# Products of constants in the gaps of TensorE: routing, the first expert, and the norms of the third block

## The reference, cut to what matters

```
x = layer_norm(ALPHA * x + mixer(x), ln1_g, ln1_b)         # second block
# routing: 4 groups, the best 2 of the 8 experts of the best group
lg = x @ wg + bg;  le = x @ we + be;  w = softmax(top 2) * p_top
# each of 32 experts, on the rows that chose it
y[rows] += ((silu(x[rows] @ w1) * (x[rows] @ w3)) @ w2) * w
x = layer_norm(ALPHA * x + y, ln2_g, ln2_b)
h = rms_norm(x, norm_gain_3);  proj = h @ w_in_3           # third block
```

## Time and profile before

| | us |
|---|---|
| median of 3 runs | 3408.27 (3405.32 to 3410.0) |
| the profiled execution, its own time | 3407.77 |
| its span in the profile | 3406.0 |
| routing, from the barrier to the next one | about 2373.9 to 2422.6 |
| third block's norms, barrier to first product | about 3019.4 to 3059.2 |

### The profile page before, as it was taken

The page is one execution under the profiler, slowest core; times in us unless marked ns, Lnnn a source line. Parts: engine busy times, 40 slices in busy tenths (PEclk is TensorE's granted clock), DMA queues, the critical chain, the costliest instruction groups (busy, mean ns, idle before and its releaser), DMA issues. The chain is left out here.

```text
span 3406.0 us, 34603 instructions
## 1 busy us (share of the span) xinstructions
PE 3016.5 (89%) x11712; PEld 1972.7 (58%) x11712; DVE 2402.0 (71%) x4782; ACT 1395.6 (41%) x2332; POOL 700.2 (21%) x583
## 2 busy tenths in 40 slices
PE   7999999977787777777789999997699999949999
PEld 4676644433333333333357898776588888837777
DVE  4888566667777776777759765545688889864675
ACT  2334222222222222222235423443488888853764
POOL 0000133344444444444410000000022212100000
PEclk9999999999999999899899999999799999969999
DMA  8432399999999999999962211343799999942212
GB/s 289 136 87 97 138 380 391 393 402 421 421 419 418 409 419 421 411 416 411 415 253 81 63 44 53 109 161 106 270 358 373 377 372 371 368 148 56 62 44 75
DMA packets 351924, 905.87 MB, mean 266 GB/s; under 512 B 29826, under 2 KB 170626, under 8 KB 285571
## 3 DMA queue, kind: packets, MB, share of 16 engines
q0 software_dynamic: 84000, 549.52, 39.5%
q1 hardware_dynamic: 267746, 354.11, 30.5%
HBM read 896.71 MB, written 31.99 MB: 273 GB/s over the span
## 5 line engine op out<-in xcount | busy, mean ns | idle before, releaser
L257 PE MATMUL peer_acc<-peer_uv,peer_diag 128*128 128x512 f32 x2048 | 992.9, 637 | 240.8 <-ACT peer_diag L313 238.4
L257 PEld LDWEIGHTS peer_acc<-peer_uv,peer_diag 128*128 128x128 f32 x2048 | 407.1, 203 | 808.0 <-issue 485.8
L434 DVE CUSTOM_DVE_ANT_0 peer_uv<-peer_uv,firsts_h 128x1024 f32<-128x1024 f32 x512 | 627.9, 1228 | 343.2 <-DMA peer_uv<-in_peer_uv,peer_experts 340.9
L208 POOL DMA_INDIRECT peer_uv<-in_peer_uv,peer_experts x512 | 575.6, 1124 | 1153.7 <-PE peer_acc L257 716.7
L3074 DVE TENSOR_TENSOR slotted_low<-slotted_raw,slotted_high 128x2048 fp32r<-128x2048 f32 x192 | 434.2, 2289 | 65.0 <-ACT slotted_high L3023 64.9
L3023 ACT ACTIVATE slotted_high<-slotted_raw 128x2048 fp32r<-128x2048 f32 x192 | 365.6, 1921 | 62.5 <-PE slotted_h L2980 50.2
L313 ACT ACTIVATE peer_diag<-all_consts,peer_weights 128x128 f32<-128x128 f32 x512 | 166.7, 391 | 333.1 <-DVE peer_weights L427 301.4
L304 ACT ACTIVATE peer_act_in<-peer_act_in 128x4 f32<-128x4 f32 (+2 forms) x131 | 26.8, 205 | 607.1 <-DVE peer_act_in L434 607.1
L2980 PE MATMUL slotted_h<-slotted_high,slotted_xT_high 128*128 128x512 f32 x512 | 204.7, 400 | 6.2 <-DVE slotted_low L3074 4.1
L2980 PE MATMUL slotted_h<-slotted_high,slotted_xT_low 128*128 128x512 f32 x512 | 201.6, 394 | 0.0
L2980 PE MATMUL slotted_h<-slotted_low,slotted_xT_high 128*128 128x512 f32 x512 | 201.2, 393 | 0.0
(11 more groups left out here) (758 smaller groups left out, 5597.4 us busy)
## 6 DMA issues: line engine op xcount, KB each, us to landing
slotted_raw<-in_moe_w SPq DMA_DIRECT2D x192, 1024.0 KB, 8.6
mixers_raw<-in_w_in SPq DMA_DIRECT2D x56, 512.0 KB, 3.8
firsts_ada_raw<-in_w_ada SPq DMA_DIRECT2D x64, 256.0 KB, 2.8
third_raw<-in_w_in SPq DMA_DIRECT2D x30, 512.0 KB, 3.6
firsts_raw<-in_w_in SPq DMA_DIRECT2D x28, 512.0 KB, 4.0
firsts_ada_first<-in_w_ada SPq DMA_DIRECT2D x8, 1024.0 KB, 13.9
peer_uv<-in_peer_uv,peer_experts POOLq DMA_INDIRECT x512, 10.7
ffn_w_raw<-in_peer_wq SPq DMA_DIRECT2D x10, 512.0 KB, 20.5
```

The lines of the kernel that those rows point to most:

```text
L208: pool.indirect_dma_start(uv[:, n % R, :, :].rearrange("p a d -> p (a d)"), None, A["peer_uv"], bass.IndirectOffsetOnAxis(ap=experts[:, si ...
L257: mm = nc.tensor.matmul(acc[t % 2][j][:, :], diag[:, n % 4, :], uv[:, n % R, 1, j * BANK:(j + 1) * BANK], start=(m == 0), stop=(m == E - 1))
L434: nc.vector.tensor_tensor_reduce(uv[:, n % R, 0, :], uv[:, n % R, 0, :], h2[:, t, :], 1.0, 0.0, ALU.mult, ALU.add, act_in[:, side, i:i + 1 ...
```

## The change

A helper multiplies two constant tiles of 128x128, `ones` and `ident`, into the first 128 columns of a bank `n` times. No one reads the result. Calls with fixed counts stand between the steps of TensorE.

```diff
+def idle_products(nc, C, bank, n):
+    for _ in range(n):
+        nc.tensor.matmul(bank[:, 0:P], C["ones"], C["ident"], start=True, stop=True)
 def routing(...):     # rows_tensor
             yield float(n)
+            if half == 0:
+                idle_products(nc, C, banks[n], (50, 8, 8, 14)[t])
             pe.wait_ge(x_ready, t + 1)
...                    # router_tensor
         yield 40.0
+        pe.wait_ge(x_low, 1)
+        idle_products(nc, C, banks[0], 14)
         pe.wait_ge(x_low, 2 * NT)
...
         tr.then_inc(lg_turned, 1)
+        idle_products(nc, C, banks[5], 36)
         pe.wait_ge(hits_ready, 1)
...
+        idle_products(nc, C, banks[5], 28)
         pe.wait_ge(at_ready, 1)
...                    # slotted_experts, TensorE
+                idle_products(nc, C, ps_x[0], 26)
                 turn_x(0)
+                idle_products(nc, C, ps_h[0], 10)
                 for e in range(NE):
...                    # third_block, rows_tensor
                 yield -100.0 + n
+                if n == 0:
+                    pe.wait_ge(x_added, 3)
+                    idle_products(nc, C, all_banks[n], 30)
+                    pe.wait_ge(x_ready, 1)
+                    idle_products(nc, C, all_banks[n], 36)
+                    pe.wait_ge(x_ready, 2)
+                if half == 0:
+                    idle_products(nc, C, all_banks[n], (8, 20, 24, 8)[t])
                 pe.wait_ge(rows_normed, t + 1)
...
                 tr.then_inc(rows_turned, 1)
+            pe.wait_ge(h_low, 1)
+            idle_products(nc, C, all_banks[0], 14)
```

## The result

The changed kernel takes 3418.9 us (median of 17 runs, 3412.77 to 3423.75) against 3408.45 us of the kernel before (17 runs, 3402.68 to 3413.25): ratio 1.0032, with an interval of 1.0026 to 1.0039, so 0.3% slower. (A ratio is taken over all runs of both kernels and can differ a little from that of the two medians.) The forecast was 3415.8, in a range from 3409.5 to 3421. The profiled execution spans 3416.8 us, 10.8 more than that of before.

What follows compares the result with a forecast made beforehand. The prediction took TensorE to be the bound behind both places, waiting in routing and the third block's norms. It added +8.1 (norms), +0.7 (routing, first expert) and -0.8 (pause) to 3407.8: 3415.8 us, range 3409.5 to 3421.

Steps and rivals of the forecast that it cites:

- The price of a product: All helper calls: one f32 product of constants is two instructions, 0.2225 us at full clock and 0.445 at the low one.
- The rival by which they fit: All filled gaps: products cheap enough to end in time, below 0.147 us in the third block; 3397 to 3403 us, chance 0.11.
- The third block's norms: Third add to block's first product: 140 products, 32 transposes and cold start take 37.2 us, 10.6 late; net +8.1.
- The cold start: Start of the third block's norms: about 5 us at low clock lose 2.5 us of work, between 1.7 and 3.4.
- the warm start: Third block's first 14 products: at full clock they take 3.2 us instead of 5.62, a gain of 2.4.
- The last tile's norm: Third block's norms: it ends at 3055.54 and is needed at about 3065.9, so it delays nothing.
- Routing and the first expert: From the barrier through the first expert: it starts 3.2 us late, its products gain 2.5; net +0.7, between -0.7 and +1.9.
- The cold start of 1.4 us in routing: Products ahead of the router: loss if the clock falls over the pause at the barrier, between 0 and 1.7 us.
- The credit of 0.8 us for the pause behind the first expert: Wait for weights behind the first expert: half of the clock fall's cost of about 1.5 us taken back, -0.8.
- the +1.9 for routing and the first expert: Upper bound on the net loss of routing and the first expert, forecast at +0.7 us.
- Products that don't lift the clock: All places: each product costs 0.445 us, third block +43, routing about +50, near 3500 us; chance 0.04.
- A late start that is taken up later: Third block: little lateness is regained; with routing at its best and an early clock about 3410 us; chance 0.05.

Runs made afterwards that it cites:

- The run with 74 products: Kernel before plus only the third block's products, without the first 30 and next 36 of 140: 3412.5 us, ratio 1.0014.
- The run of routing alone: Changed kernel without the third block's 140 products; routing and the first expert keep theirs in unchanged counts: 3409.8 us, ratio 0.9999.
- the fitted third block: Kernel before plus only the third block's products, 80 instead of 140, in counts that fit its pauses: 3408.7 us, ratio 1.0001.
- that with transposes: Changed kernel with each product of constants replaced by a transpose of the same tile, same counts: 3399.3 us, ratio 0.997.

## Why the prediction was right

Its price, its mechanism and its places held. The measured 10.5 us over the median of before are 3 us more than the forecast's 7.5, for the reasons below.

- **The price of a product.** 0.2225 us each: in the trace, 40 instructions lead from 3056.85 to 3061.32, 0.112 us each, so 0.2235. The rival by which they fit needed under 0.147.
- **The third block's norms.** 37.2 us were forecast, +10.6; the trace has 37.48, +10.85. The cold start in it took about 2.7 us, for 2.5. In the trace the warm start gave back 2.6, for 2.4: from the first to the fourteenth product of the block 3.06 us, for 5.62. The times don't confirm that term (see above). The run with 74 products confirms the sum in another form (32.0 forecast, 31.88 measured).
- **A reading that was wrong and did no harm.** "The last tile's norm, at 3054.26 + 1.28 = 3055.54, is needed at about 3065.9" takes that norm's time from the trace before. But VectorE's list has low parts, which wait for the transposes, ahead of the last norm, so it moved with them: 11.3 us later, of which the later third add (3036.65 for 3032.60) explains 4.1.

```profile
3065.58 1.28 DVE L3426 SCALAR_TENSOR_TENSOR third_hn<-all_x,third_squared_sums,last_rows 128x1024 f32<-128x1024 f32 x1
```

  It ends at 3066.86, 3.3 us ahead of the last transposes at 3070.21. The slack was a third of the 10 us that the prediction gave it.
- **Routing and the first expert.** Forecast and trace: end of the counting products 2415.4, and the helper's next group begins at 2415.28; end of the rows' products 2423.4 and 2421.54 + 1.95 = 2423.49; first transposes 2430.8 and 2430.97; the first expert 3.2 us late and 3.36. The cold start of 1.4 us in routing, taken between 0 and 1.7, was there: 100 instructions in 12.64 us, 1.5 more than at 0.1115 each. From its start to the pause behind it the first expert took 17.87 us for 20.12, 2.25 less (2.5 forecast). The run of routing alone, at 0.9999, agrees that lateness and clock cancel.
- **The credit of 0.8 us for the pause behind the first expert failed.** The step was "Whether it does depends on how the pause lies; I take half of it back": the clock fell there in the changed kernel too (0.84), and in all nine traces that leave this pause unfilled, though it is moved by up to 10 us; only the three that fill it don't have it. The pause itself (4.11 us) decides, not its place. What the fall costs varies: 6 to 13 products stand 0.43 us apart instead of 0.23, 1.2 to 2.6 us.
- **What the sum left out.** The changed trace has a fall of the clock at the last down products (0.75 over 6.9 us, about 1.6 us) that before had not, a third add that ends 1.4 us later (25.06 for 23.69), and no later fall in the block (before had one, 1.7). The change doesn't touch these, and they vary between the kernels above (23.69 to 26.97 us for the leg of the pause). Together they make +1.2 in this pair; with the credit's 0.8 and 0.7 in the forecast's own terms (0.2 to 0.3 each in the start of the first expert, its products and the norms) that is the difference between the forecast's +8.0 and the 10.8 between the two spans, to 0.1. Three unforeseen terms of 1.4 to 1.7 us each cancel in part (1.6 and 1.4 against 1.7); that the forecast came within 3 us is luck to that extent. The medians are 10.5 apart; the interval reaches down to 8.9, so it leaves the forecast's 7.5 out.
- **Bounds without a row.** The 3.4 us for the cold start and the +1.9 for routing and the first expert follow from no row that is named; with 1.7 for the cold start in routing the second would be +1.0. The cold starts of the norms took 2.0 to 2.7 us in the traces that have all 140 products.
- **The rivals.** Products that don't lift the clock: excluded by 1.00 over the 31 us from 3043. Products that fit: excluded by 0.2235 us each and a norms leg of 37.48 us for 26.63. A late start that is taken up later: the rest was 4.1 us shorter, but by the warm start (about 2.4) and the missing fall (1.7), both of which are clock, not regained lateness.

The range from 3409.5 to 3421 held the time. What the prediction didn't weigh is how near the gain was: the same products in about two thirds of the number turn +10.5 us into -8.8.

## What to carry to other kernels

A pause on TensorE could be filled with products of constants at no cost that these runs can tell, and the work behind it then ran at full clock; here that was worth 7.5 us (4.4 to 10.6) in routing and the first expert, and 3 us of the trace in the experts' own pauses. Price the filler from a row of the same form and type (an f32 product is two instructions), and size each group to end just ahead of the step that it waits beside. In the trace a short bracket in front of a real step shows that the filler ends early enough; where there is none, compare the step's start with that in the kernel before, or the filler may have become the bound. Against a fixed wait only the overhang counts, and behind the last wait every product counts in full.

## What the runs showed of the hardware

- Some of the clock's falls vary from trace to trace without a change in the code there, at 1.6 to 1.9 us each. The fall at the last expert's down products, behind a pause of 2.18 us, is missing in the traces of before and of the fitted third block and present in seven others without a fill there. Two kernels that differ by less than about 3 us are not told apart by one trace each.
- Here TensorE's f32 transposes raised the clock (0.50, then 1.00, under nothing else) and held it as products do, at half the time per call.
- The third add's end (the leg of the pause, 23.69 to 26.97 us) hangs on when the results' loads land: VectorE's first wait for them is 4.83 us before, 5.78 in the changed kernel and 6.73 in that with transposes, whose legs are 23.69, 25.06 and 26.97.
